# A two-layer decoder step on one Trainium2 core: queries of the other tokens by rows from weights already in the ring, and the samples' second-layer projections in four quarters of a PSUM bank

## The chip, the cores and the metric

The program runs on one core of a Trainium2 chip. The metric is the device time of one execution in microseconds (us): 2491.01 us as the median of three runs before the change (2483.01 to 2494.72). The names of the engines in the rows are PE (TensorE, the matrix engine; PEld is its weight load, that is, the loading of the stationary operand), DVE (VectorE), ACT (ScalarE), POOL (GpSimd, which here issues the gathers of the experts' rows) and SP (SyncE, which issues the other loads and the stores). All data are 32-bit floats. A 32-bit matrix multiplication stands in the trace as two PE records, a transpose as one.

## What is computed

256 prompt tokens and 8 x 4 sample tokens go through two layers with width 1024. Layer 0 mixes by a gated recurrence and sparse attention, layer 1 by dilated attention; each is followed by an expert layer, whose routing is the part that matters here:

```python
def peer_ffn(x, w_q, sub_keys, u, v):                 # 16 blocks of 128 query columns
    q = (xt @ w_q).reshape(n, PEER_HEADS, 2, PEER_QDIM // 2)      # w_q: 1024 x 2048
    s = jnp.einsum('nhcd,hckd->nhck', q, sub_keys)                # scores against 128 keys
    s1, i1 = lax.top_k(s[:, :, 0], PEER_TOPK); s2, i2 = lax.top_k(s[:, :, 1], PEER_TOPK)
    ...                                               # 16 of the 16 x 16 pairs, for each of 8 heads
    eidx = jnp.take_along_axis(cidx, sel, axis=-1); gate = jax.nn.softmax(top, axis=-1)
    ...                                               # 128 experts a token: gelu(u[e].x) * gate, times v[e]

def odd_project(x, pos, w_in):                        # layer 1: w_in is 1024 x 3072
    h = (x @ w_in).reshape(B, T, 3, DIL_HEADS, HEAD_DIM)
    return rope(h[:, :, 0], pos), rope(h[:, :, 1], pos), h[:, :, 2]
```

## The kernel before, in words

The tokens are three tiles: two of 128 prompt tokens (tiles 0 and 1) and one of 32 samples (tile 2). `k.x` holds them by rows, `k.xT` transposed: eight chunks of 128 of the width on the partitions, the tokens along the free axis (samples first). A projection multiplies chunk by chunk and sums eight chunks in a PSUM bank.

The program has three parts. First comes the mixer of layer 0 up to its output projection and normalisation (`even_out`). The second part is the routing of tile 0. It is two blocks with a barrier behind each: in the first, `project_cols` makes the queries of tile 0 (`peer_q0`); in the second, `route` scores and selects for tile 0 on DVE (`first_route`), while `project_cols` makes the queries of the samples and of tile 1 (`rest`, named `peer_q12`). `project_cols` keeps the *weights* stationary: for each of 16 blocks of 128 query columns and each chunk it loads a 128x128 piece of the weights and streams 32 or 128 tokens against it; the result is already transposed, as `route` wants it (`peer_qT`), and leaves by a copy, in `rest` by ACT alone. The weights lie in the eight slots of the experts' ring (`uv`, 1 MB each); `rest` loads all eight again. In this block ACT runs its part of `rest` first and then the one exponential of `first_route` (`scalar=(rest, first_route)`), for which DVE waits before it can finish the softmax, the expert numbers (`slots`) and the gates. PE runs the scores of `first_route`, then `rest`.

The third part is one long block, in which the 576 expert steps run in the foreground and everything else beside them. A step gathers 128 rows of 8 KB, one for each token, into a ring of eight slots (L1769, issued by POOL), takes the dot products on DVE (L1787), scales a diagonal on ACT and multiplies it into the sum on PE (L1879, four records), or, for some of the steps, sums on DVE (L1801). The slot is free when the sum has read it. The side work (routings of the other tiles, and per tile a `mixer`: layer 1's projection, rotation, attention and output, then the projection of the layer-1 queries) is cut into ticks with weights; `WINDOWS` says between which steps each runs, and the ticks of a window are spread over its steps in proportion to their weights. The instructions of an engine therefore stand in one fixed order, expert steps and side ticks mixed, and each waits for the one ahead of it. A side stage ends on a barrier of the four engines with SP, and SP issues the loads of the next stage before it lets them on.

In `mixer 2` (the samples; steps 408 to 498) the stages that concern us are: `project_wide` with the samples (32 tokens) stationary, which streams 512 columns of weights at a time into six banks of 32 used partitions (L502), twelve loads of 1 MB; `rotate_and_store`, which rotates queries and keys in four pieces of 32x512 (L706 to L711) and stores keys and values; `transposes` of sixteen 32x128 blocks; then four attention stages over the cached keys and values, the output projection, and `late_routing`, which projects the samples' queries with `project_wide` again (eight loads of 1 MB, four banks) and transposes sixteen blocks.

Of the kernel before, what the change touches and what calls it, by code (L numbers as in the profile page):

```python
# [32 lines left out]
D = 1024  # L33
KC = D // 128
# [189 lines left out]
def cols(t):  # L224
    return slice(COL0[t], COL0[t] + ROWS[t])
# [296 lines left out]

def project_cols(k, name, w, n, outT, wbuf, toks=(slice(0, NTOK),), banks=ALL_BANKS, by=("vector", "scalar")):
# [62 lines left out]
    for side, engine in enumerate(by):  # L586
        stage.on(engine)(lambda eng, side=side, engine=engine: take_out(eng, side, outs[side], copies[engine]))
    return stage
# [1400 lines left out]
def dilated_tile(k, name, t, a, o, val, kT):  # L1989
# [5 lines left out]
    with ExitStack() as outer:  # L1995
# [3 lines left out]
        with ExitStack() as inner:  # L1999
            qk = k.sbuf(name + "_qk", [128, 1, 2 * D], ctx=inner)  # L2000
            with ExitStack() as load:
# [5 lines left out]
                stages.append(project_wide(k, name + "_in", a["odd_w_in"][0], ((0, 2 * D), (2 * D, D)), out, wbuf, t, SIDE_BANKS))  # L2007
            with ExitStack() as rot:
                tmp = k.sbuf(name + "_tmp", [128, 4, 256], ctx=rot)
                stages.append(rotate_and_store(k, name + "_rot", qk, val, tiles, o["dil_p"], o["dil_s"], tmp))  # L2010
            groups = [([qk[0:r, 0, at + 128 * (c + j):at + 128 * (c + j + 1)] for j in range(4)], dst[:, c:c + 4, cols(t)])
                      for dst, at in ((qT, 0), (kT, D)) for c in range(0, HP, 4)]
            stages.append(transposes(k, name + "_qk", groups, SIDE_BANKS))
# [26 lines left out]
def late_routing(k, name, t, a, route_tile):  # L2040

    r = ROWS[t]
    with ExitStack() as late:
        qT = k.sbuf(name + "_qT", [128, 2 * PH, r], ctx=late)
        keysT = k.sbuf(name + "_keysT", [128, 2 * PH, NK], ctx=late)
        with ExitStack() as load:
# [4 lines left out]
            stages = [turn_keys(k, name + "_keys", a["peer_sub_keys"][1], keys, keysT, SIDE_BANKS),  # L2051
                      project_wide(k, name + "_q", a["peer_w_q"][1], ((0, 2 * PH * 128),), lambda j: rows[0:r, 512 * j:512 * (j + 1)],
                                   wbuf, t, SIDE_BANKS),
                      transposes(k, name + "_qT", [([rows[0:r, 128 * (4 * i + j):128 * (4 * i + j + 1)] for j in range(4)],
                                                    qT[:, 4 * i:4 * i + 4, :]) for i in range(4)], SIDE_BANKS)]
# [32 lines left out]
def build(nc, a, o):  # L2088
    with ExitStack() as whole:
# [6 lines left out]
        with ExitStack() as ctx:  # L2096
# [16 lines left out]
            with ExitStack() as first:  # L2113
# [60 lines left out]
```

## Time and profile before

| | |
|---|---|
| median of three runs | 2491.01 us |
| the runs | 2483.01 to 2494.72 us |
| span of the profiled execution, first to last instruction | 2536.6 us |
| mean granted TensorE clock | 0.845 of 2.4 GHz |
| busy: PE, DVE, ACT, POOL | 77%, 58%, 22%, 29% |
| moved by DMA | 759.29 MB, mean 299 GB/s |

The profiled execution has no time of its own beside its span here; the span is 45.6 us (1.8%) longer than the median of the runs without the profiler. Busy shares are means over stages with different limits, so the page is read by stage: its second part cuts the span into 40 slices of 63.4 us. PEclk is the granted clock in tenths of 2.4 GHz, and DMA is the busy share of the 16 DMA engines; up to 1.02 stands for full in the windows, where they move about 420 GB/s.

### The profile page before, as it was taken

To read this page: it belongs to the slowest core of one execution; us is meant where nothing else is said; L and a number is where in the kernel's file an instruction comes from. 1 tells how busy PE (TensorE), PEld (TensorE's weight loads), DVE (VectorE), ACT (ScalarE), POOL (GpSimd) and SP (SyncE) were. 2 spreads that over 40 slices of the span, in tenths; PEclk is the share of its full clock that TensorE was granted. 3 is DMA by queue.
4 is the path that set the end of the run, shared out by engine and by line. 5 is a ranking of instruction groups with operands and counts; after the bars stand their busy time and mean duration, and the time that the engine had idled before them with its cause. 6 is when DMAs were issued, how large, how long until landed. Compare 5 with 4: busy or idle time off the path is not lost.

```text
span 2536.6 us, 20142 instructions
## 1 busy us (share of the span) xinstructions
PE 1965.3 (77%) x6151; PEld 987.9 (39%) x6151; DVE 1470.2 (58%) x3338; ACT 559.8 (22%) x1759; POOL 728.6 (29%) x612
## 2 busy tenths in 40 slices
PE   7968289889877877886869768677978687878776
PEld 3456255569833322222324223233422255623221
DVE  0043632128078777657755973585594565456976
ACT  0010222000022322224322231142221122212231
POOL 4000000000044455433444452233442132223442
PEclk9985556685599999998989988888999787789988
DMA  8200100524199999999999999799999799889997
GB/s 277 91 17 1 37 1 0 152 81 133 40 422 421 421 421 422 399 419 359 401 413 421 415 395 420 307 384 383 406 393 405 278 359 349 325 329 384 402 385 306
DMA packets 160436, 759.29 MB, mean 299 GB/s; under 512 B 22204, under 2 KB 63048, under 8 KB 80328
## 3 DMA queue, kind: packets, MB, share of 16 engines
q0 software_dynamic: 84480, 608.21, 59.0%
q1 hardware_dynamic: 75848, 149.80, 16.4%
q8 instruction: 49, 0.80, 0.1%
q14 instruction: 59, 0.48, 0.1%
HBM read 752.35 MB, written 5.60 MB: 299 GB/s over the span
## 4 chain that ended last, share of the span: by engine, by line
DMA 23%; PE 20%; DVE 17%; issue 6%; ACT 2%; SPq 1%; PEld 1%; POOL 1%; PEldq 1%; DVEq 1%; ACTq 0%; POOLq 0%
DMA uv<-in_experts_dram,slots 16%; PE ps L1879 9%; DVE uv L1787 6%; PE ps L502 4%; PE ps L824 2%; DMA sample_cache<-in_odd_w_in_dram 1%; PE ps L796 1%; DMA last_w<-in_odd_w_in_dram 1%; DMA sample_w<-in_peer_w_q_dram 1%; PE ps L657 1%; POOL uv L1769 1%; SPq L1494 1%; PEldq L1915 1%; DVE acc L1801 1%; ACT diag L1855 1%
## 5 line engine op out<-in xcount | busy, mean ns | idle before, releaser
L1769 POOL DMA_INDIRECT uv<-in_experts_dram,slots x576 | 698.0, 1212 | 1746.5 <-PE ps L1879 1000.9
L1879 PE MATMUL ps<-uv,diag 128*128 128x512 f32 (+1 forms) x1880 | 973.5, 659 | 271.1 <-ACT diag L1855 211.9
L1787 DVE CUSTOM_DVE_ANT_0 uv<-uv,x 128x1024 f32<-128x1024 f32 x512 | 623.0, 1225 | 307.3 <-DMA uv<-in_experts_dram,slots 253.8
L1879 PEld LDWEIGHTS ps<-uv,diag 128*128 128x128 f32 (+1 forms) x1880 | 349.2, 198 | 813.3 <-issue 469.2
L1833 ACT ACTIVATE gelu<-dot 128x2 f32<-128x2 f32 x288 | 58.6, 203 | 1051.4 <-DVE dot L1787 1045.9
L1855 ACT ACTIVATE diag<-const,wgt 128x128 f32<-128x128 f32 (+1 forms) x470 | 165.0, 387 | 9.4
L1842 ACT ACTIVATE wgt<-gate,gelu 128x1 f32<-128x1 f32 x576 | 138.0, 286 | 48.2 <-SPq L1982 14.4
L563 PE MATMUL ps<-xT,uv 128*128 128x128 f32 (+1 forms) x768 | 139.0, 367 | 1.6 <-DMA uv<-in_peer_w_q_dram 1.6
L563 PEld LDWEIGHTS ps<-xT,uv 128*128 128x128 f32 x768 | 138.7, 287 | 1.8 <-DMA uv<-in_peer_w_q_dram 1.8
L1801 DVE SCALAR_TENSOR_TENSOR acc<-uv,wgt,acc 128x1024 f32<-128x1024 f32 x101 | 129.3, 1280 | 1.5 <-ACT wgt L1842 1.5
L1787 DVE CUSTOM_DVE_ANT_0 uv<-uv,xs 128x1024 f32<-128x1024 f32 x64 | 78.0, 1225 | 74.7 <-DMA uv<-in_experts_dram,slots 73.3
L425 PE MATMUL ps<-even_w,xT 128*128 128x512 f32 (+3 forms) x240 | 99.0, 565 | 6.1 <-issue 4.9
L502 PE MATMUL ps<-last_w,xT 128*128 128x512 f32 x160 | 76.2, 620 | 13.4 <-DMA last_w<-in_odd_w_in_dram 12.5
L502 PE MATMUL ps<-first_w,xT 128*128 128x512 f32 x160 | 75.4, 611 | 2.9 <-DMA first_w<-in_odd_w_in_dram 2.9
L425 PEld LDWEIGHTS ps<-even_w,xT 128*128 128x128 f32 (+1 forms) x240 | 38.0, 165 | 66.7 <-issue 62.6
L440 DVE COPY h<-ps 128x512 f32<-128x512 f32 (+3 forms) x8 | 5.0, 626 | 89.6 <-PE ps L425 56.5
L502 PEld LDWEIGHTS ps<-last_w,xT 128*128 128x128 f32 x160 | 30.8, 196 | 55.7 <-issue 36.2
L502 PE MATMUL ps<-sample_cache,xT 128*32 128x512 f32 x96 | 46.1, 627 | 8.1 <-DMA sample_cache<-in_odd_w_in_dram 8.1
L657 PE MATMUL ps<-even_w_out,xT 128*128 128x512 f32 (+1 forms) x96 | 44.3, 624 | 6.5 <-DMA even_w_out<-in_even_w_out_dram 6.5
L878 DVE COPY xT<-ps 128x256 f32<-128x256 f32 (+3 forms) x19 | 6.8, 360 | 72.1 <-PE ps L824 72.0
L502 PEld LDWEIGHTS ps<-first_w,xT 128*128 128x128 f32 x160 | 29.7, 193 | 47.7 <-issue 41.4
L824 PEld LDWEIGHTS ps<-sample_s_probT,sample_cache 128*128 128x128 f32 x256 | 47.4, 290 | 2.1 <-issue 2.1
(409 smaller groups left out, 1911.6 us busy)
## 6 DMA issues: line engine op xcount, KB each, us to landing
uv<-in_peer_w_q_dram SPq DMA_DIRECT2D x16, 1024.0 KB, 11.9
sample_cache<-in_cache_dil_kv_dram SPq DMA_DIRECT2D x64, 256.0 KB
first_w<-in_odd_w_in_dram SPq DMA_DIRECT2D x12, 1024.0 KB
last_w<-in_odd_w_in_dram SPq DMA_DIRECT2D x12, 1024.0 KB, 12.0
sample_cache<-in_odd_w_in_dram SPq DMA_DIRECT2D x12, 1024.0 KB, 15.6
uv<-in_experts_dram,slots POOLq DMA_INDIRECT x576
even_w<-in_even_w_in_dram SPq DMA_DIRECT2D x8, 1024.0 KB, 8.4
first_w<-in_peer_w_q_dram SPq DMA_DIRECT2D x8, 1024.0 KB, 9.7
```

Source lines behind the costliest of these rows:

```text
L425: last = nc.tensor.matmul(k.bank(banks[i % nb])[0:ROWS[t], 0:widths[j]], k.xT[:, 4 * half + c, cols(t)], wbuf[:, load % slots, c, 0:widths ...
L502: last = nc.tensor.matmul(k.bank(banks[job])[0:r, :], k.xT[:, chunk, cols(t)], wbuf[:, i % slots, width * c + 512 * j:width * c + 512 * (j ...
L563: last = nc.tensor.matmul(k.bank(banks[i % nb])[:, place], wbuf[:, j % slots, c, 128 * (i % 2):128 * (i % 2 + 1)], k.xT[:, c, tok], start= ...
L657: last = nc.tensor.matmul(bank(n, h)[0:ROWS[t], :], catT[:, 2 * i + c, cols(t)], w[:, i % slots, c, 512 * h:512 * (h + 1)], start=(i == 0 ...
L824: last = nc.tensor.matmul(out, lhsT, pick(probT[0:kn, r % 2, :]), start=start, stop=stop, skip_group_check=True)
L1769: self.k.nc.gpsimd.indirect_dma_start(out=self.uv[:, s % RING, :], out_offset=None, in_=self.table, in_offset=bass.IndirectOffsetOnAxis(ap ...
L1787: ins = nc.vector.tensor_tensor_reduce(self.uv[:, s % RING, 0:D], self.uv[:, s % RING, 0:D], x, 1.0, 0.0, ALU.mult, ALU.add, self.dot[:, g ...
L1801: nc.vector.scalar_tensor_tensor(self.acc[:, :], v, w, self.acc[:, :], ALU.mult, ALU.add).then_inc(self.added, 1)
L1833: nc.scalar.activation(self.gelu[:, grp % 2, :], self.dot[:, grp % 2, :], ACT.Gelu).then_inc(self.gelued, 1)
L1842: ins = nc.scalar.activation(self.wgt[:, grp % 2, g:g + 1], self.gate[:, t, j:j + 1], ACT.Copy, scale=self.gelu[:, grp % 2, g:g + 1])
L1855: last = nc.scalar.activation(self.diag[:, step % RING, 0:w], k.c(shape), ACT.Copy, scale=self.wgt[:, grp % 2, g:g + 1])
L1879: last = nc.tensor.matmul(k.bank(c)[0:m, :], self.diag[:, s % RING, 0:m], self.uv[:, s % RING, D + 512 * c:D + 512 * (c + 1)], start=(j == ...
```

## The change

There are two parts.

In the routing of tile 0, `rest` becomes `queries_by_rows`. It loads nothing: the weights that `peer_q0` left in the ring are used. The *tokens* are now stationary. Tile 1 takes 32 multiplications with 512 columns into banks 4 to 7 (four banks of rows, eight chunks each). The samples take 32 multiplications of 32 stationary columns and 512 streamed ones, all into bank 4: the four quarters of the query columns go to the partitions 0 to 31, 32 to 63, 64 to 95 and 96 to 127, chunk by chunk with the four quarters next to each other. ACT copies the five results to SBUF; PE turns them by 16 and 4 transposes of 128x128; ACT copies those to `peer_qT`, four copies and four.

In `mixer 2` and in the late routing of the samples, `project_wide` becomes `project_quarters` in the same manner: queries and keys of layer 1 (2048 columns) go to four quarters of one bank by 32 multiplications with 512 columns, the values (1024 columns) to four quarters of a second bank by 32 with 256, and the late queries to one bank by 32 with 512. The loads are the same twelve and eight of 1 MB. The rotation runs once over 128x512, the keys and values leave by three stores, and four transposes of 128x128 with eight small copies take the place of sixteen transposes with four copies. The ticks and weights of these stages change with them.

```diff
+def project_quarters(k, name, w, groups, leaves, wbuf, banks):
...
+    stage = Stage(k, len(ticks), 1.4)
...
+                for q in range(4):
+                    last = nc.tensor.matmul(k.bank(banks[g])[NS * q:NS * (q + 1), 0:n], k.xT[:, chunk, SMP],
+                                            wbuf[:, i % slots, width * c + n * q:width * c + n * (q + 1)],
+                                            start=(chunk == 0), stop=(chunk == KC - 1), skip_group_check=True)
...
+def turn_quarters(k, name, rows, outs, banks):
...
+        for m in range(4):
+            last = nc.tensor.transpose(k.bank(banks[m // 2])[:, 128 * (m % 2):128 * (m % 2 + 1)], rows[:, 128 * m:128 * (m + 1)],
+                                       k.c("ident"))
...
+def rotate_and_store_quarters(k, name, qk, val, out_s, tmp):
...
+        rotate(k, qk[:, :], qk[:, :], (2, 128), HEADS // 2, tmp)
...
+        for j in range(2):
+            k.store(sp, dst[:, 0, 512 * j:512 * (j + 1)], qk[NS * (2 + j):NS * (3 + j), :])
+        k.store(sp, dst[:, 1, :], val[0:NS, 2, :])
+        k.wait_for_stores(sp)
...
+def queries_by_rows(k, name, wbuf, rows, quarters, qT):
...
+        for j in range(4):
+            for c in range(KC):
+                last = nc.tensor.matmul(wide(4 + j), k.xT[:, c, cols(1)], wbuf[:, 2 * j:2 * j + 2, c, :], start=(c == 0), stop=(c == KC - 1))
+            last.then_inc(made, 1)
+        pe.wait_ge(taken, 1)
+        for c in range(KC):
+            for q in range(4):
+                last = nc.tensor.matmul(wide(4, slice(NS * q, NS * (q + 1))), k.xT[:, c, SMP], wbuf[:, 2 * q:2 * q + 2, c, :],
+                                        start=(c == 0), stop=(c == KC - 1), skip_group_check=True)
+        last.then_inc(made, 1)
+        for i, b in enumerate((5, 6, 7, 4)):
+            pe.wait_ge(taken, i + 2)
+            for j in range(4):
+                last = nc.tensor.transpose(k.bank(b)[:, 128 * j:128 * (j + 1)], rows[:, 512 * i + 128 * j:512 * i + 128 * (j + 1)], ident)
+            last.then_inc(made, 1)
...
+        for j in range(4):
+            act.wait_ge(made, j + 1)
+            copy(rows[:, 512 * j:512 * (j + 1)], k.bank(4 + j)).then_inc(taken, 1)
...
-                    first_route, rest = r(0, 0, qT, keysT, load, None), project_cols(
-                        k, "peer_q12", a["peer_w_q"][0], 2 * PH * 128, qT, wbuf, (SMP, cols(1)), (4, 5, 6, 7), ("scalar",))
+                    rows = k.sbuf("peer_rows", [128, 2 * PH * 128], ctx=load)
+                    quarters = k.sbuf("peer_quarters", [128, 512], ctx=load)
+                    first_route = r(0, 0, qT, keysT, load, None)
+                    rest = queries_by_rows(k, "peer_q12", wbuf, rows[:, :], quarters[:, :], qT)
                     alone(k, first_route, rest, scalar=(rest, first_route))
```

On PE, in the block of the first routing, the program before has this behind the scores (`peer_keysT,peer_qT`); the last two rows stand 32 times in turn. The first row is tile 0's queries, the branches are the barrier; `uv` is the ring, `xT` the tokens.

```order
L563 MATMUL ps<-xT,uv 128x128 x128
L274 UNCONDITIONAL_BRANCH
L275 UNCONDITIONAL_BRANCH
L1573 MATMUL ps<-peer_keysT,peer_qT 128x128 x16
L563 MATMUL ps<-xT,uv 128x32 x4
L563 MATMUL ps<-xT,uv 128x128 x4
```

The same place on PE now:

```order
L692 MATMUL ps<-xT,uv 128x128 x128
L274 UNCONDITIONAL_BRANCH
L275 UNCONDITIONAL_BRANCH
L1756 MATMUL ps<-peer_keysT,peer_qT 128x128 x16
L736 MATMUL ps<-uv,xT 128x512 x32
L741 MATMUL ps<-uv,xT 32x512 x32
L747 MATMUL ps<-const,peer_rows 128x128 x16
L751 MATMUL ps<-const,peer_quarters 128x128 x4
```

256 multiplications and 16 hand-overs to ACT have become 64 and 20 transposes.

On ACT, in the same block, what stands ahead of the exponential of the first routing (`route_e`) is now this; before it were 32 copies of 128x32 and 128x128.

```order
L760 COPY peer_rows<-ps 128x512 x4
L762 COPY peer_quarters<-ps 128x512
L765 COPY peer_qT<-ps 128x4x128 x4
L768 COPY peer_qT<-ps 128x4x32 x4
L1777 ACT_TABLE_LOAD
L1777 ACTIVATE route_e<-route_e 128x128
```

The exponential still stands behind the whole of `rest`.

On DVE, in `mixer 2`, the rotation of the samples (`sample_qk` with `sample_tmp`) before stood in four pieces, two of them between expert steps (`uv,dot<-uv,x` is a step's dot product); the first piece and the step behind it:

```order
L706 TENSOR_TENSOR sample_tmp<-sample_qk,const 32x256
L707 TENSOR_TENSOR sample_tmp<-sample_qk,const 32x256
L708 TENSOR_TENSOR sample_tmp<-sample_qk,const 32x256
L709 TENSOR_TENSOR sample_tmp<-sample_qk,const 32x256
L710 TENSOR_TENSOR sample_qk<-sample_tmp 32x8x32
L711 TENSOR_TENSOR sample_qk<-sample_tmp 32x8x32
L1787 ISA uv,dot<-uv,x 128x1024
L1787 ISA dot 128x1
```

Now it is one piece, and what follows is this (the step's two `ISA` rows stand twice there and are shown once):

```order
L893 TENSOR_TENSOR sample_qk<-sample_tmp 128x8x32
L894 TENSOR_TENSOR sample_qk<-sample_tmp 128x8x32
L638 MEMSET progress 128x1
L1970 ISA uv,dot<-uv,x 128x1024
L1970 ISA dot 128x1
L1984 SCALAR_TENSOR_TENSOR acc<-uv,wgt,acc 128x1024
L620 COPY sample_qT<-ps 128x64 x2
L620 COPY dil_kT<-ps 128x2x32 x2
```

24 rotation instructions became six, and the expert steps that lay between them moved: on DVE 429 dot products stood ahead of the first copy of the turned cache keys (`sample_s_kTs`), now 426, and each of the four attention stages has 13 steps where it had 12.

## Rows read from the trace of the kernel before

**Rows 1.** The page's second part: DMA in 40 slices of the span.
```profile
DMA  8200100524199999999999999799999799889997
```
**Rows 2.** Windows by stage; columns: stretch, length, busy by engine, clock, DMA share, GB/s.
```profile
510.00:523.00 13.00, 13.00 (x32) 3.40 (x32) 6.40 (x9) 0.20 (x1) 0.00 (x0) 1.00 1.00 320
553.00:571.00 18.00, 17.39 (x156) 17.23 (x155) 1.46 (x5) 1.32 (x5) 0.00 (x0) 1.00 0.00 1
...
587.00:685.00 98.00, 98.00 (x460) 97.98 (x460) 38.28 (x146) 4.95 (x28) 0.00 (x0) 0.50 0.11 34
```
**Rows 3.** Timeline of DVE, first routing; columns: start, us, engine, line, operation, [idle before].
```profile
626.12 0.29 DVE L1663 TENSOR_TENSOR route_e<-route_top 128x128 f32<-128x128 f32 x1
687.31 0.29 DVE L1666 TENSOR_REDUCE route_den<-route_e 128x8 f32<-128x128 f32 x1 [60.90 <-ACT route_e L1594]
```
**Rows 4.** Timeline of ACT, end of the first routing's block.
```profile
685.68 1.28 ACT L1594 ACT_TABLE_LOAD   x1
686.97 0.31 ACT L1594 ACTIVATE route_e<-route_e 128x128 f32<-128x128 f32 x1
```
**Rows 5.** Timeline of PE, first routing's block.
```profile
570.88 3.81 PE L1573 MATMUL ps<-peer_keysT,peer_qT 128*128 128x128 f32 x32 [0.61 <-PEq L274]
576.30 108.97 PE L563 MATMUL ps<-xT,uv 128*128 128x32 f32 x512 [1.62 <-DMA uv<-in_peer_w_q_dram]
```
**Rows 6.** Timeline of PE: 512 columns against 32, and transposes, at full clock.
```profile
1930.21 5.34 PE L502 MATMUL ps<-sample_cache,xT 128*32 128x512 f32 x12
...
2078.44 1.91 PE L348 MATMUL ps<-const,sample_cache 128*128 128x128 f32 x16
```
**Rows 7.** Timeline of PE: neighbours that write different halves of the partitions.
```profile
245.21 1.97 PE L1114 MATMUL ps<-hg_v_b,hg_keyT 32*64 32x512 f32 x4
...
1681.37 1.13 PE L824 MATMUL ps<-last_p_probT,dil_val 128*64 128x128 f32 x8 [3.59 <-ACT last_p_probT L899]
```
**Rows 8.** The clock in the windows of rows 7.
```profile
245.20:247.20 2.00, 1.98 (x5) 0.29 (x4) 0.00 (x0) 0.00 (x0) 0.00 (x0) 0.50 0.00 0
...
1681.00:1682.60 1.60, 1.23 (x9) 0.90 (x10) 0.87 (x2) 1.58 (x2) 0.00 (x0) 0.50 1.00 415
```
**Rows 9.** Groups by line and form: copies, rotation; columns: busy, mean ns.
```profile
L359 ACT COPY sample_s_kTs<-ps 128x512 f32<-128x512 f32 x16 | 9.1, 571 | 3.9 <-PE ps L348 2.3 <-issue 1.6
...
L707 DVE TENSOR_TENSOR sample_tmp<-sample_qk,const 32x256 f32<-32x256 f32 x4 | 1.7, 420 | 0.0
```
**Rows 10.** Windows of mixer 2; columns as in rows 2.
```profile
1940.00:1960.00 20.00, 17.15 (x39) 3.93 (x37) 3.66 (x5) 1.09 (x4) 4.07 (x4) 1.00 1.01 419
...
1980.00:2000.00 20.00, 13.87 (x27) 4.15 (x24) 16.13 (x32) 4.13 (x11) 4.58 (x5) 0.83 0.36 127
2000.00:2020.00 20.00, 8.32 (x23) 4.19 (x24) 15.10 (x30) 2.79 (x11) 4.05 (x4) 0.59 0.86 310
...
2040.00:2200.00 160.00, 131.32 (x545) 85.97 (x545) 93.90 (x159) 39.28 (x110) 46.24 (x40) 0.80 0.91 352
...
2300.00:2320.00 20.00, 14.97 (x46) 4.78 (x44) 8.20 (x13) 3.49 (x12) 5.97 (x6) 1.00 0.85 330
1900.00:2340.00 440.00, 342.99 (x1099) 165.64 (x1098) 247.86 (x439) 95.60 (x279) 119.22 (x104) 0.84 0.88 346
```
**Rows 11.** Timeline of PE around the samples' rotation.
```profile
1984.42 3.62 PE L502 MATMUL ps<-sample_cache,xT 128*32 128x512 f32 x8
...
2026.81 1.96 PE L348 MATMUL ps<-const,sample_cache 128*128 128x128 f32 x8 [5.75 <-SPq L1982]
```
**Rows 12.** Timeline of SP's queue there.
```profile
1963.79 0.37 SPq L476 DMA_DIRECT2D sample_cache<-in_odd_w_in_dram  x1
...
2011.68 3.98 SPq L336 DMA_DIRECT2D sample_cache<-in_cache_dil_kv_dram  x8
2015.71 10.94 SPq L1494 DMA_DIRECT2D sample_cache<-in_cache_dil_kv_dram  x8
```

**Rows 13.** The page's sixth part: issue, KB, median us from issue to landing.
```profile
sample_cache<-in_odd_w_in_dram SPq DMA_DIRECT2D x12, 1024.0 KB, 15.6
```

More of the change, by code:

```diff
@@ new lines, in turn_quarters, with _, take_out @@
+def turn_quarters(k, name, rows, outs, banks):
+    nc = k.nc
+    turned, v_out, s_out = [k.sem(name, n) for n in ("turned", "v_out", "s_out")]
+    stage = Stage(k, 2, 1.5)
+    sides = ((v_out, nc.vector.tensor_copy), (s_out, nc.scalar.copy))
+    @stage.on("tensor")
+    def _(pe):
+        for m in range(4):
+            last = nc.tensor.transpose(k.bank(banks[m // 2])[:, 128 * (m % 2):128 * (m % 2 + 1)], rows[:, 128 * m:128 * (m + 1)],
+                                       k.c("ident"))
+            if m % 2:
+                last.then_inc(turned, 1)
+        yield
+        yield
+    def take_out(eng, side):
+        done, copy = sides[side]
+        yield
+        eng.wait_ge(turned, side + 1)
+        for first, n, dst in outs:
+            src = k.bank(banks[side])[:, 0:256].rearrange("p (m j t) -> p j m t", m=2, t=NS)
+            for j in range(n):
+                last = copy(dst[:, 4 * j + 2 * side:4 * j + 2 * side + 2, :], src[:, first + j])
+        last.then_inc(done, 1)
+        yield
+    stage.on("vector")(lambda dve: take_out(dve, 0))
+    stage.on("scalar")(lambda act: take_out(act, 1))
+    return stage
@@ L1999, in dilated_tile @@
         with ExitStack() as inner:
-            qk = k.sbuf(name + "_qk", [128, 1, 2 * D], ctx=inner)
+            qk = k.sbuf(name + "_qk", [128, 1, 512 if t == 2 else 2 * D], ctx=inner)
             with ExitStack() as load:
@@ L2050, in late_routing @@
             keys = rows[:, :].rearrange("p (a b) -> p a b", b=128)
[L2051 to L2055, printed above, removed]
+            turned = turn_keys(k, name + "_keys", a["peer_sub_keys"][1], keys, keysT, SIDE_BANKS)
+            if t == 2:
+                quarters = rows[:, 0:512]
+                stages = [turned, project_quarters(k, name + "_q", a["peer_w_q"][1], ((0, 2 * PH * 128),), ([(quarters, slice(0, 128), 512)],),
+                                                   wbuf, SIDE_BANKS),
+                          turn_quarters(k, name + "_qT", quarters, [(0, 2, qT[:, 0:8, :]), (2, 2, qT[:, 8:16, :])], SIDE_BANKS)]
+            else:
+                stages = [turned,
+                          project_wide(k, name + "_q", a["peer_w_q"][1], ((0, 2 * PH * 128),), lambda j: rows[0:r, 512 * j:512 * (j + 1)],
+                                       wbuf, t, SIDE_BANKS),
+                          transposes(k, name + "_qT", [([rows[0:r, 128 * (4 * i + j):128 * (4 * i + j + 1)] for j in range(4)],
+                                                        qT[:, 4 * i:4 * i + 4, :]) for i in range(4)], SIDE_BANKS)]
         with ExitStack() as inner:
```

116 lines of the change are left out of this document (111 added, 5 removed).

## The prediction

> **What bounds the kernel now.** I read the page's slices first [rows 1]. From slice 12 on, DMA stands at 9 nearly throughout: the expert steps run at the rate of their gathers there, and a faster PE buys nothing. Two kinds of holes matter. One lies ahead of the experts, in slices 10 and 11 (571 to 698 us), where DMA is at 4 and 1: the first routing. The others lie at slices 32, 35 and 36 (7, 8 and 8), in mixer 2. The windows then price both. In the first routing PE is busy all of 98 us at a clock of 0.50, while DVE works 38 [rows 2]. The timelines show who ends last: DVE has route_e at 626.4 and stands 60.90 us for ACT's exponential [rows 3]; ACT comes to it only behind the last copy of `rest`, at 685.7 [rows 4]; and ACT was kept by PE, whose 512 records run from 576.30 to 685.27 [rows 5]. Nothing else runs, and POOL's first gather stands behind the barrier. So that block ends by PE, and every us taken from PE there is a us of the kernel, until DVE's own end.
>
> In mixer 2 the DMA share is 1.01 while most of the weights come in, then 0.36 and 0.86 around the rotation, 0.91 in the attention stages and 0.85 at the end of the late queries [rows 10]. Over the 440 us it is 0.88 against the 1.01 of full, so (1.01 - 0.88) x 440 = 57 us of DMA time are unused. This is all that the second part of the change can win.
>
> **Part one: the first routing.** The reload of 8 MB and its wait of 1.62 us at 576.30 go. PE is free at 570.88 + 3.81 = 574.7 [rows 5]. What a record costs: 512 columns against 32 stationary ones at full clock take (5.34 - 0.2) / 12 = 0.427 us (0.2 being the last one's tail, my estimate), a transpose (1.91 - 0.2) / 16 = 0.107 us [rows 6]. The width of the stationary side does not enter: on the 98 us a 32-column stream costs as much as a 128-column one, 108.97 / 512 = 0.213 us at half clock [rows 5], which is 0.427 for 256 such columns and so agrees with 0.427 for 512 at full clock.
> - Tile 1: 32 multiplications, 64 records x 0.427 = 27.3 us, to 602.0.
> - Samples: 64 records. One after the other they would be 27.3 us too; four at a time 16 x 0.427 = 6.8 us, to 608.9. Before has no case of four, but of two. Four records of 512 columns at half clock (0.85 us each, 3.4 in a row) took 1.97 us there, and eight of 128 (0.213 each, 1.7) took 1.13, these with all 128 rows of the array in use [rows 7], both at a clock of 0.50 [rows 8]. So pairs that write different partitions overlap nearly whole. Bounds: 6.8 and 27.3 us; I take 6.8, since both pairs halve.
> - The end: behind the quarters a copy of the samples' rows, then four to `peer_qT`, 0.571 us each [rows 9], in ACT's order, then four small copies of about 0.3: 0.2 + 5 x 0.57 + 1.1 = 4.2 us, to about 613. The 20 transposes (2.1 us, 4.3 at half clock) lie beside the copies.
>
> DVE is not touched and has route_e at 626.4. `rest` then ends 13 us under that cover. The table load of 1.28 us stood ahead of the wait, not behind it [rows 4], so it is done by then too; the exponential of 0.31 us follows at once, and DVE goes on at about 626.8 instead of 687.31. Gain: 60.5 us. What is late next is DVE itself. The bounds come from the clock and the overlap, in the rivals below.
>
> The Trainium skill has a rule against this (TensorE: Matmul & The Clock Gate, "Part 3: Packing small matmuls"): weight loads overlap running multiplications only when the row group differs, and the quarters share all rows. The trace disagrees: neighbours with the same rows overlap [rows 7]. The same section gives 2.38x for three column tiles; with it as an estimate the samples would take 27.3 / 2.38 = 11.5 us, and the sum would be the same, since 4.7 us more fit under DVE.
>
> **Part two: mixer 2 and the samples' late queries.** 160 records x 0.427 = 68.3 us on PE (96 and 64 of them) become 17.1 if four overlap. Most of it buys nothing, because the DMA is full there. What the chain gives:
> - Projection. The last piece of weights is asked for at 1963.79; its multiplications end at 1984.42 + 3.62 = 1988.0 [rows 11, 12]. A piece takes 15.6 us to land [rows 13], so it is there at about 1979.4. What is left behind it, at a quarter of its length and with an expert step between, ends near 1982: -6 us. Bounds 0 (the norm of the expert layer that falls there binds) and -10.
> - Rotation: 24 instructions x 0.41 become 6 [rows 9]; DVE does 128 partitions in the time of 32. 18 x 0.41 = -7.4 us on the chain, since PE and the cache loads wait for it. Bounds -5 and -10 (two expert steps between the pieces go too).
> - Transposes behind it: 0. They are fewer, but SP issues the keys' and values' loads from 2011.68 until 2026.65 in any case [rows 12], and PE goes on at 2026.81, when SP lets it [rows 11]. This wait takes the place of what is saved. The third store goes beside the others: 0.4 us.
> - Late queries: DMA is full up to 2300, then 0.85 for 20 us [rows 10]: -4 us, bounds 0 and -8.
> - Moved steps: each attention stage now has 13 expert steps for 12. PE works 131 of 160 us there and DMA has a share of 0.91 [rows 10], so a step (1 MB, 2.5 us of DMA) fits in part: +1 us a stage, +4 in all; bounds 0 and +8.
>
> Sum, rounded: -6 - 7 - 4 + 4 = -13 us, bounds -28 (all lower ends) and +3 (all upper ends).
>
> **The forecast.** -60.5 - 13 = -73.5 us. Against the profiled execution that is 2536.6 - 73.5 = 2463 us of span. The runs without profiler are 1.8% shorter; PE at a fixed clock should not depend on that, so I take the us as they are: 2491.0 - 73.5 = 2417.5, rounded to 2417 us.
>
> **The rivals.**
> 1. The quarters run one after the other. This is what the skill's rule would make of them here. For it: no row shows four at once, each streaming over all 128 rows. Against: the pairs [rows 7]. `rest` then ends at 613 + 20.5 = 634, 7.5 us behind DVE, a gain of 53 us. In mixer 2 only rotation and the ends remain, about -9. 2491 - 53 - 9 = 2429 us.
> 2. The clock falls to 1.2 GHz (0.50) in the block of the first routing. For it: before it was 0.50 there over 98 us of unbroken PE work, behind 1.00 in the stage ahead [rows 2]. Against: that work was 128- and 32-column streams; with 512-column streams of 32 stationary columns the clock was 1.00 [rows 2], as in mixer 2's projection [rows 10]. With overlap: 574.7 + 54.6 + 13.7 + 6 = 649, 22.5 us late, gain 38: 2491 - 38 - 13 = 2440 us.
> 3. Part two gives nothing, since the DMA in front of and behind the hole takes the time back: 2491 - 60.5 = 2430 us. For it: rows 10 with DMA full on both sides; against: the 0.36 in the middle.
> 4. The other side: quarters in a row and at half clock, everywhere. `rest` ends at 574.7 + 54.6 + 54.6 + 7 = 691, 5 us later than before; in mixer 2 160 records at 0.85 instead of 0.43 add 68 us to a PE that is busy 17 of 20 us [rows 10], some +50. 2491 + 5 + 50 = 2546 us. In the first block the sign turns where a record takes over 0.8 us in the mean, (685 - 575 - 7) / 128. Both conditions together have [rows 2, 7] against them.
>
> **Chances.** Forecast (overlap, full clock, part two between -5 and -28) 0.62; rival 1 0.10; rival 2 0.09; rival 3 0.16; rival 4 0.03. The likeliest's own range is 2402 to 2426; with the rivals 1 to 3 and what the profiled execution cannot tell, the range is 2398 to 2439. Under 0.5% (12 us) this kernel cannot be told from no change. Cases 1 to 3 and the forecast are all faster by more: 0.95 faster; a partial form of rival 4 could land within: 0.03; slower 0.02.
>
> **What would show it.** In the changed profile: DVE's idle before the reduction of route_e under 1 us (60.90 before), and the first gather some 60 us earlier; the 32-column records of the first routing ending four by four within about 0.9 us of each other, and the clock 1.00 there; no loads of peer_w_q in that block; the samples' projection ending some 18 us after its last piece is asked for instead of 24; one rotation of 2.5 us; the window between projection and first cache keys shorter by some 13 us, the DMA share of 0.36 gone. The forecast is wrong if DVE waits for ACT by more than 5 us (rival 1 or 2, told apart by clock and spacing), or if mixer 2's window is as long as before (rival 3).

## The result, and the profile after

| | before | after |
|---|---|---|
| median, 19 runs each side by side | 2501.21 us | 2474.75 us |
| lowest to highest | 2483.01 to 2552.04 | 2468.65 to 2488.82 |
| span of the profiled execution | 2536.6 us | 2474.0 us |
| PE records | 6151 | 5795 |

2417 us had been forecast, with a range of 2398 to 2439; the changed kernel takes 2474.75. The kernel before has two groups of runs: 10 of the 19 lie from 2483 to 2501 us, 9 from 2529 to 2552. The changed kernel has one. Against the lower group alone the change is 0.6% faster: the ratio is 0.9939, with an interval of 0.9922 to 0.9956, which is 15 us (11 to 19). The profile shown ahead of the prediction is one execution of the upper group, and everything below turns on it.

The page of the changed kernel, its slices of the clock and of DMA (compare [rows 1]):

```profile
PEclk9986556699899999988899989898997776778988
DMA  8200100340999999989999999899999988889997
```

The first routing on PE (compare [rows 5]), ACT [rows 4] and DVE [rows 3], and its window [rows 2]:

```profile
565.20 3.81 PE L1756 MATMUL ps<-peer_keysT,peer_qT 128*128 128x128 f32 x32 [0.61 <-PEq L274]
568.85 27.63 PE L736 MATMUL ps<-uv,xT 128*128 128x512 f32 x64
```
```profile
L741 PE MATMUL ps<-uv,xT 128*32 128x512 f32 x64 | 7.1, 594 | 0.0
```
```profile
606.02 0.82 ACT L768 COPY peer_qT<-ps 128x128 f32<-128x128 f32 x4
606.86 1.28 ACT L1777 ACT_TABLE_LOAD   x1
620.75 0.31 ACT L1777 ACTIVATE route_e<-route_e 128x128 f32<-128x128 f32 x1 [12.61 <-DVE route_e L1846]
```
```profile
620.42 0.29 DVE L1846 TENSOR_TENSOR route_e<-route_top 128x128 f32<-128x128 f32 x1
621.09 0.29 DVE L1849 TENSOR_REDUCE route_den<-route_e 128x8 f32<-128x128 f32 x1 [0.38 <-ACT route_e L1777]
```
```profile
565.00:610.00 45.00, 40.62 (x180) 19.80 (x180) 40.83 (x205) 6.92 (x14) 0.00 (x0) 1.00 0.00 1
```

The experts' gathers fill the slices from number 11 on, one slice earlier. Inside this block every step came as forecast. The samples' records start four at a time, 5 to 8 ns after one another, with some 410 ns between one four and the next. Tile 1 takes 27.6 us, the samples' 64 records 7.1 (forecast 6.8), the clock is 1.00, ACT stands 12.61 us for DVE (forecast 13 under cover), and DVE's idle of 60.90 us is 0.38. Against the profiled execution of before, 60.5 us are gone, and yet the runs gained 15.

### The profile page after: what moved, and what is told of

Its sections match the earlier page's. It is cut to its first block, busy times and chain, and to the rows that moved or that the text cites. A ratio compares the mean times of both kernels' runs of the same rounds, so it can differ in the third digit from the quotient of the medians.

```text
span 2474.0 us, 19380 instructions
## 1 busy us (share of the span) xinstructions
PE 1858.3 (75%) x5795; PEld 889.4 (36%) x5795; DVE 1463.7 (59%) x3323; ACT 557.7 (23%) x1741; POOL 720.7 (29%) x612
## 4 chain that ended last, share of the span: by engine, by line
DMA 26%; PE 21%; DVE 17%; issue 5%; ACT 2%; SPq 1%; POOL 1%; PEldq 1%; DVEq 1%; PEld 0%; ACTq 0%; POOLq 0%
DMA uv<-in_experts_dram,slots 18%; PE ps L2062 11%; DVE uv L1970 6%; PE ps L502 3%; PE ps L1007 2%; DMA sample_cache<-in_odd_w_in_dram 2%; DMA last_w<-in_odd_w_in_dram 2%; PE ps L979 2%; PE ps L840 1%; DMA sample_w<-in_peer_w_q_dram 1%; DVE acc L1984 1%; ACT diag L2038 1%; DVE route_ef L1841 1%; DMA out_dil_p_dram<-dil_val 1%; POOL uv L1952 1%
## 5 line engine op out<-in xcount | busy, mean ns | idle before, releaser
L1952 POOL DMA_INDIRECT uv<-in_experts_dram,slots x576 | 690.1, 1198 | 1692.2 <-PE ps L2062 1017.7
L1007 PEld LDWEIGHTS ps<-sample_s_probT,sample_cache 128*128 128x128 f32 x256 | 52.6, 317 | 3.3 <-issue 3.3
L1007 PE MATMUL ps<-sample_s_probT,sample_cache 128*128 128x8 f32 x256 | 51.5, 345 | 0.0
L1034 DVE TENSOR_TENSOR nsa_prob<-ps,const 128x512 f32<-128x512 f32 (+3 forms) x16 | 10.2, 640 | 68.6 <-PE ps L979 68.6
L1970 DVE DVE_READ_ACCUMULATOR2_ANT dot<- 128x1 f32 x576 | 47.2, 82 | 0.0
L979 PE MATMUL ps<-sample_s_kTs,sample_q_b 128*64 128x256 f32 x128 | 35.1, 429 | 15.9 <-DVE sample_q_b L1685 15.9
```

Source lines behind the costliest of these rows:

```text
L979: last = nc.tensor.matmul(score_bank(i)[p0:p0 + pn, c0:c0 + cn], lhsT, rhs, start=start, stop=stop)
L1007: last = nc.tensor.matmul(out, lhsT, pick(probT[0:kn, r % 2, :]), start=start, stop=stop, skip_group_check=True)
L1952: self.k.nc.gpsimd.indirect_dma_start(out=self.uv[:, s % RING, :], out_offset=None, in_=self.table, in_offset=bass.IndirectOffsetOnAxis(ap ...
L1970: ins = nc.vector.tensor_tensor_reduce(self.uv[:, s % RING, 0:D], self.uv[:, s % RING, 0:D], x, 1.0, 0.0, ALU.mult, ALU.add, self.dot[:, g ...
```

## The experiments

Each kernel ran on one chip beside runs of the kernel before. A run over 2515 us is called long and the others short: among the 94 runs of the kernel before none lies between 2507 and 2525 us.

### Where the 60 us are

Four kernels, the kernel before again among them (its expectation has the two counts of the 19 runs exchanged). `p1_only` is part one of the change alone, `p2_only` part two alone. `no_reload` is the kernel before without its second 8 MB of loads and the waits for them:

```diff
-        for j in range(slots):
+        for j in range(0 if kept else slots):
             load(sp, j)
...
-            if i % 2 == 0:
+            if i % 2 == 0 and not kept:
                 pe.wait_ge(landed[j % slots], 16 * (j // slots + 1))
```

> The kernel before, unchanged, to get the profile of one of its shorter executions. Its 19 runs fall in two groups, 9 of 2483 to 2501 us and 10 of 2529 to 2552 us; the profile shown (2536.6 us) is of the longer group. Theory A (clock in the first routing): in the shorter group the queries of the samples and of tile 1 run at a granted clock of 1.00, the 512 PE records take 55 to 60 us in place of 108.97 us, DVE waits 2 to 15 us in place of 60.90, and the loop of the experts behind it is as long as in the shown profile (1847 us within 5). Theory B (the loop): the clock of that block is 0.50 in every run, and the 45 us lie in the loop of the experts, which is then about 1800 us.

> The kernel before without the second load of the 8 MB of layer 0's query weights: the same instructions on PE, with no wait for a load. It tells what brings the low clock in that block. Theory A1 (the waits for the reload, in which PE stands still, let the clock fall): all runs in the shorter group, clock 1.00 in the block, about 2484 us. Theory A2 (the stream itself, 128x128 pieces of weights against 32 and 128 columns in turn, does not hold the clock): two groups of runs as before, or all in the longer one. Theory B: no difference from before.

> The changed kernel with the second part undone (dilated_tile and late_routing as before): queries by rows only. Theory A: against the shorter runs of before it gains what `rest` ends behind DVE at full clock, 5 to 10 us: 2479 to 2485 us, and no run in a longer group. Theory B (part one is worth its 60 us in every run, part two costs about 45 us): 2425 to 2435 us. If part two gives nothing in the loop, this kernel is as long as the whole change, 2475 us within 5.

> The changed kernel with the first part undone (the first routing as before): quarters in the samples' second-layer projections only. Theory A: two groups of runs as before, the shorter one within 5 us of before's shorter one (2485 to 2495 us). Theory B: part two costs about 45 us, 2535 us and more against the shorter runs of before. My forecast had -13 us for this part (2476 us in the shorter group).

The kernel before, another execution of it (span 2481.1 us), in PE's and DVE's timeline (compare [rows 5] and [rows 3]) and in a window of the same stage (compare [rows 2]):

```profile
564.10 3.81 PE L1573 MATMUL ps<-peer_keysT,peer_qT 128*128 128x128 f32 x32 [0.61 <-PEq L274]
569.43 57.44 PE L563 MATMUL ps<-xT,uv 128*128 128x32 f32 x512 [1.52 <-DMA uv<-in_peer_w_q_dram]
```
```profile
628.91 0.28 DVE L1666 TENSOR_REDUCE route_den<-route_e 128x8 f32<-128x128 f32 x1 [9.31 <-ACT route_e L1594]
```
```profile
590.00:600.00 10.00, 10.00 (x92) 10.00 (x91) 9.69 (x53) 1.06 (x6) 0.00 (x0) 1.00 0.02 5
```

The same 512 records took 57.44 us at a clock of 1.00 where they had taken 108.97 at 0.50, and DVE waited 9.31 us instead of 60.90. These 51.5 us are most of the 55.5 us between the spans. Another 6.8 lie ahead of the scores (564.10 against 570.88), 5.5 of them ahead of tile 0's queries and 1.3 in these, and the loop behind gives 3 back. So the two levels of the clock in this block make the difference between this short execution and the long one. The runs that have no profile show their mean clock alone, and it parts them in the same way: it is 0.855 to 0.867 in 25 short runs of before, and 0.835 to 0.849 in 49 long ones. In the lower group part one can give 9.31 - 0.38 = 8.9 us.

| kernel | runs to 2515 us: n, median | runs from 2515 us |
|---|---|---|
| before, 11 runs here | 2, 2497.2 | 9 |
| before_again | 3, 2489.8 | 3 |
| p1_only | 6, 2486.6 | 0 |
| p2_only | 5, 2480.6 | 1 |
| no_reload | 6, 2486.2 | 0 |

`no_reload` computes with the same narrow streams and has no long run; in its profile the 512 records take 57.34 us at a clock of 1.00.

### What of the reload lets the clock fall

The reload is a wait of 1.5 us at the start of the block, and a traffic of 8 MB behind it. `reload_first` loads and awaits piece 0 alone, `reload_late` pieces 3 to 7, which PE reaches some 20 us later; `reload_two` waits for two pieces at the start. They differ from the kernel before in

```diff
-        for j in range(slots):
+        for j in range(slots) if loaded is None else loaded:
             load(sp, j)
...
-            if i % 2 == 0:
+            if i % 2 == 0 and (loaded is None or j in loaded):
                 pe.wait_ge(landed[j % slots], 16 * (j // slots + 1))
+                if loaded is not None and j == 0:      # reload_two alone
+                    pe.wait_ge(landed[1], 16)
```

with `loaded` (0,), (3, 4, 5, 6, 7) and (0, 1) for `peer_q12`. `after_wait` is the changed kernel with 1 MB reloaded and awaited ahead of its first multiplication:

```diff
+        sp.dma_start(wbuf[:, 0, :, :], w_first).then_inc(landed, 16)
...
+        pe.wait_ge(landed, 16)
         for j in range(4):
             for c in range(KC):
```

> The kernel before, whose second making of queries loads only the first of its eight pieces again (1 MB) and waits for it alone: the wait of PE at the start of it stays (1.5 us), the traffic of the other 7 MB goes. Theory A1 (the wait makes the clock fall in some executions): two groups again, about half of six runs over 2515 us, the others near 2488. A2 (the traffic of 8 MB does): no run over 2500. A3 (neither; what differs lies ahead of this block, and the absence of long runs without the reload was chance): two groups.

> The kernel before, whose second making of queries loads the last five of its eight pieces again (5 MB), which PE comes to some 20 us later: traffic stays, the wait of PE at the start goes. A1 (the wait makes the clock fall): no run over 2500 us, all near 2486. A2 (the traffic does) or A3 (neither): two groups, about half of the six runs over 2515 us. With the run beside it: only the first in two groups is A1, only the second A2, both A3, neither means that it takes both or that the cause is rarer than six runs show.

> The kernel before, loading the first two pieces again and waiting for both before the first multiplication: the wait of PE at that place grows from 1.5 us to about 4. With one piece 4 of 6 runs were long. Theory A1 (the wait there is what lets the clock fall): at least as many long runs, 4 to 6 of 6 over 2530 us. Rival (a wait of any length is not the cause, and 0 of 18 without it was chance): no more than 2 of 6.

> The changed kernel, whose second making of queries loads the first 1 MB of the weights again and lets PE wait for it, as before did: one wait of 1.5 to 1.8 us on PE between the scores and the first multiplication; the other traffic stays away. Theory A1 (that wait makes the clock fall to 0.50 for the rest of the block in more than half of the executions, whatever PE multiplies): two groups of runs. Where the clock stays, the wait lies under DVE's 12.6 us of cover and the run takes the changed kernel's 2475 us; where it falls, the 64 records of tile 1 take 54.6 us and the quarters 14, ACT's exponential comes 20 to 28 us behind DVE's need, and the run takes 2495 to 2505 us, about half of the six runs. Rival (the clock falls only under streams of 32 and 128 columns): all six at the changed kernel's time.

| kernel | PE's wait there | streams | long runs of all |
|---|---|---|---|
| before, five sets of runs | 1.62 and 1.52 us | 32 and 128 columns | 58 of 93 |
| p2_only, p2_beside | 1.77 and 1.53 | the same | 6 of 18 |
| reload_first | 1.50 | the same | 4 of 6 |
| reload_two | 4.67 | the same | 6 of 6 |
| no_reload, reload_late | none | the same | 0 of 6, 0 of 12 |
| after_wait | 1.69 | 512 columns | 0 of 6 |
| changed kernel, four sets of runs | none | 512 columns | 0 of 43 |
| p1_only, p1_beside | none | 512 columns | 0 of 18 |

(One more run of before, at 3165 us and a mean clock of 0.545, belongs to neither group and is left out.) `reload_two`, PE's timeline and windows (clock last but two), then DVE's:

```profile
568.44 3.81 PE L1575 MATMUL ps<-peer_keysT,peer_qT 128*128 128x128 f32 x32 [0.61 <-PEq L274]
576.91 109.57 PE L565 MATMUL ps<-xT,uv 128*128 128x32 f32 x512 [4.67 <-DMA uv<-in_peer_w_q_dram]
```
```profile
565.00:575.00 10.00, 6.64 (x58) 6.28 (x56) 4.09 (x11) 0.27 (x1) 0.00 (x0) 1.00 0.57 175
575.00:580.00 5.00, 3.09 (x14) 3.12 (x15) 4.83 (x31) 0.00 (x0) 0.00 (x0) 0.68 0.22 69
580.00:600.00 20.00, 20.00 (x96) 20.00 (x95) 19.38 (x115) 1.06 (x6) 0.00 (x0) 0.50 0.00 1
600.00:680.00 80.00, 80.00 (x378) 80.00 (x376) 23.28 (x59) 4.20 (x24) 0.00 (x0) 0.50 0.00 1
```
```profile
688.52 0.28 DVE L1668 TENSOR_REDUCE route_den<-route_e 128x8 f32<-128x128 f32 x1 [64.59 <-ACT route_e L1596]
```

And `reload_first` and `p2_only`, in profiled executions that are short ones, with waits of the same length:

```profile
567.52 57.44 PE L563 MATMUL ps<-xT,uv 128*128 128x32 f32 x512 [1.50 <-DMA uv<-in_peer_w_q_dram]
568.24 57.44 PE L692 MATMUL ps<-xT,uv 128*128 128x32 f32 x512 [1.77 <-DMA uv<-in_peer_w_q_dram]
```

The long runs need the wait and not the traffic: with 5 MB of traffic and no wait at the start none of 12 is long, with 1 MB and the wait 4 of 6 are. That a longer wait makes more of them is likely but not shown: at the rate of before, six of six would come by chance once in 17 times. The long runs take the narrow streams too: the rival to A1 in `after_wait` held, six runs of 2466 to 2481 us. (A fall shorter than DVE's 12.6 us of cover would not show in them.) So part one removes the long runs twice over. The Trainium skill also has a clock that falls where PE waits for a DMA (TensorE: Matmul & The Clock Gate, "HAM oscillation — how this bites in real kernels"). The waits of its example are longer than the 1.5 to 1.8 us here, so the runs agree with it in kind, and go beyond it. The picture in Part 1 of the same page, of a clock that comes back once PE is busy, does not fit here: the 109.57 us that follow are without a gap, at 0.50 to the end. Why a wait of 1.5 to 1.8 us does it in some executions and not in others stays open. Its length does not decide: the clock fell behind 1.62 us and held behind 1.77.

### The quarters, and the order of the multiplications

`serial_quarters` is the changed kernel with the two loops of the samples exchanged, for the first routing alone:

```diff
-        for c in range(KC):
-            for q in range(4):
+        for q in range(4):
+            for c in range(KC):
                 last = nc.tensor.matmul(wide(4, slice(NS * q, NS * (q + 1))), ...
```

> The changed kernel, whose samples in the first routing are multiplied quarter by quarter: all eight chunks of a quarter, then the next quarter, so that neighbours write the same partitions; the same 32 multiplications in another order. Theory Q (four neighbours overlap because they write different quarters of the partitions): the 64 records take 27.3 us where they took 7.07, ACT comes 7 to 8 us behind DVE, the first dot product and the run come 7 to 8 us later, 2482 us. Rival R (a matmul with 32 stationary columns is fast by itself, in any order): 7 us, and the changed kernel's time.

Its timelines of PE, ACT and DVE:

```profile
593.64 22.59 PE L741 MATMUL ps<-uv,xT 128*32 128x512 f32 x64
616.17 1.97 PE L747 MATMUL ps<-const,peer_rows 128*128 128x128 f32 x16
```
```profile
616.27 0.59 ACT L762 COPY peer_quarters<-ps 128x512 f32<-128x512 f32 x1 [21.94 <-PE ps L741]
```
```profile
621.25 0.28 DVE L1849 TENSOR_REDUCE route_den<-route_e 128x8 f32<-128x128 f32 x1 [3.27 <-ACT route_e L1777]
```

The same 32 multiplications take 22.59 us where they took 7.07: Q holds, and R is refuted. The size was off. I had expected 27.3 and a DVE 7 to 8 us late; it is 2.9 us later than in the changed kernel (3.27 against 0.38), and the four runs have a median of 2475.1 us against 2471.8. Why 22.59 us is 17% less than 64 x 0.427 stands in the start times of the single records. Neighbours of the same quarter start about 430 ns apart and save nothing. Around each of the three changes of quarter four records start only 6 to 30 ns behind the one ahead of them, so there too pairs ran side by side: 12 x 0.427 = 5.1 us. Against the Trainium skill's rule that weight loads overlap only between row groups (TensorE: Matmul & The Clock Gate, "Part 3: Packing small matmuls"), four neighbours that share all 128 rows run 27.3 / 7.07 = 3.9 times as fast as in a row.

### What part two gives, and where it goes

`after_again`, `after_beside` and `after_third` are the changed kernel, `p1_beside` and `p2_beside` its halves once more, all as references. `same_steps` and `same_steps_again` are the changed kernel with the weights of before for the ticks of part two, which gives each attention stage 12 expert steps again:

```diff
-    stage = Stage(k, len(ticks), 1.4)
+    stage = Stage(k, len(ticks), (25 if len(groups) == 2 else 17) / len(ticks))
...
-    stage = Stage(k, 2, 1.5)
+    stage = Stage(k, 2, 3.75)
...
-    stage = Stage(k, 1, 2.5)
+    stage = Stage(k, 1, 10.0)
```

> The changed kernel once more, on the chip of the three runs below it. Theory A (its gain lies in part in the absence of the long group of runs, and of the 12 us that part two gains by step 433 it gives back most in the attention stages): all runs in one group between 2465 and 2490 us, median about 2475, none over 2500; profile with first dot product at 631.5 us and the attention stages done at about 1412 us (step 450) to 1549 (step 480) behind it, as in its first profile. Rival (single group by chance): at least one of the six runs over 2515 us.

> The changed kernel with the ticks' weights of before in the samples' second mixer (projection 25 and 17 over its ticks, turning 3.75, rotation 10), so that the attention stages have 12 expert steps each again and stand at the same steps. Theory B (what part two gains by step 433 is given back because each attention stage got a 13th expert step): the loop is 8 to 12 us shorter than that of the changed kernel, median 2463 to 2467 us. Rival C (the DMA takes the time back whichever step stands where, since it is full in front and behind): within 4 us of the changed kernel, 2471 to 2479. Rival D (the new weights were better): slower by 5 to 10 us.

> The changed kernel beside the next three, on the same chip: 2474 to 2477 us median, no run over 2500 us.

> The changed kernel with the ticks' weights of before in the samples' second mixer, once more, beside the changed kernel. Its first six runs had a median of 2469.8 us against 2476.4 of the changed kernel on that chip. Theory B (the 13th expert step in each attention stage costs): again 5 us or more below the run beside it, 2467 to 2471. Rival C (the steps' places don't matter, the first difference was the scatter of six runs): within 3 us of the run beside it.

> The changed kernel beside its two halves on one chip, so that the 15 us between the undisturbed runs of before and of the changed kernel can be split: 2472 to 2477 us, no run over 2500.

> Part one alone (the first routing by rows, mixer 2 as before). If part two is worth 7 us (the traces' steps 408 to 500) to 12 us (the difference of the medians of other chips), this stands 7 to 12 us above the changed kernel, 2481 to 2487 us, with no run over 2515. Rival: part two gives nothing, the same as the changed kernel within 3 us.

> Part two alone (mixer 2 and the late queries in quarters, the first routing as before). Where the clock holds in the first routing, part one is worth 7.7 us by the trace (first dot product 639.2 against 631.5): the short runs stand 5 to 8 us above the changed kernel, 2480 to 2484 us; the wait at the start of the block is still there, so one or more of six runs over 2515 us.

| short runs: n, median | chip of the first halves | chip of the second |
|---|---|---|
| before (with before_again) | 5, 2495.1 | 10, 2488.2 |
| part one alone | 6, 2486.6 | 12, 2480.0 |
| part two alone | 5, 2480.6 | 7, 2486.9 (and 5 long) |
| both | not run there | 10, 2471.5 |

Part one alone gives 8.5 and 8.3 us, as the trace has it (8.9); part two alone gives 14.5 and 1.4, and on top of part one 8.5. Medians of a few runs scatter too much for it, so I took it from the traces: the loop's time from expert step 408 to 500, which holds all of mixer 2. It is 415.2 us in the mean of seven executions without part two (407.8 to 428.4) and 408.6 in eight with it and the changed weights (406.8 to 410.4): -6.6 us. This is a mean and no more. The two executions of the kernel before itself (407.8 and 409.9) lie where those with part two lie, and without the highest of the seven, `p1_only`'s 428.4 (the longest of its six runs), it is -4.4. The runs bear the size out: 11 to 19 us in all, less 8.9 for part one, leave 2 to 10.

SP's queue shows where time is won and lost. The kernel before (short execution), from the first weights of the projection to the first cache keys and the first weights of the late queries:

```profile
1860.97 47.60 SPq L476 DMA_DIRECT2D sample_cache<-in_odd_w_in_dram  x12
1949.52 0.36 SPq L175 DMA_DIRECT2D out_dil_s_dram<-sample_qk  x1
...
1954.05 3.98 SPq L336 DMA_DIRECT2D sample_cache<-in_cache_dil_kv_dram  x8
...
2206.28 35.74 SPq L476 DMA_DIRECT2D sample_w<-in_peer_w_q_dram  x8
```

On DVE, the first and last row of its rotation (24 instructions, with two steps between the pieces):

```profile
1936.96 0.41 DVE L706 TENSOR_TENSOR sample_tmp<-sample_qk,const 32x256 f32<-32x256 f32 x1
...
1948.96 0.41 DVE L711 TENSOR_TENSOR sample_qk<-sample_tmp 32x256 f32<-32x256 f32 x1
```

The same two views of the changed kernel (six instructions):

```profile
1852.74 46.80 SPq L544 DMA_DIRECT2D sample_cache<-in_odd_w_in_dram  x12
1921.44 0.82 SPq L175 DMA_DIRECT2D out_dil_s_dram<-sample_qk  x2
...
1927.52 4.67 SPq L336 DMA_DIRECT2D sample_cache<-in_cache_dil_kv_dram  x8
...
2201.80 34.08 SPq L544 DMA_DIRECT2D sample_w<-in_peer_w_q_dram  x8
```
```profile
1919.07 0.42 DVE L889 TENSOR_TENSOR sample_tmp<-sample_qk,const 128x256 f32<-128x256 f32 x1
...
1920.87 0.42 DVE L894 TENSOR_TENSOR sample_qk<-sample_tmp 128x256 f32<-128x256 f32 x1
```

From weights to cache keys it was 93.1 us and is 74.8. From there to the late queries it was 252.2 and is 274.3. Over the seven and the eight executions, and the two of `same_steps`:

| means, us | without part two | with it | same_steps, its two executions |
|---|---|---|---|
| first weights to first cache keys | 93.9 | 75.5 | 82.4, 81.1 |
| from there to the late queries | 256.3 (249.9 to 266.1) | 274.7 (272.9 to 275.8) | 268.4, 258.9 |
| from there to step 500 | 62.9 (61.0 to 68.0) | 56.5 (55.7 to 59.0) | 58.9, 60.1 |
| gathers in the first two | 17 and 60 | 15 and 64 | 17 and 60 |

So 18.4 us are won and 18.4 given back, with 79 steps in the time of 77. What is left over stands in the third stretch, which has two steps fewer and the late queries in quarters. With its steps as before (`same_steps`) it is 59.5 in the mean of two. So about half of the 6.4 us there is the late queries' and half the two steps'.

The windows of the second stretch and of 408 us from the first weights on, the kernel before and the changed kernel (columns as in [rows 2]):

```profile
1954.00:2206.00 252.00, 199.77 (x748) 120.74 (x748) 143.06 (x235) 58.12 (x166) 68.12 (x60) 0.78 0.86 330
1861.00:2269.00 408.00, 318.12 (x1020) 156.31 (x1020) 217.76 (x358) 82.80 (x244) 103.59 (x91) 0.82 0.88 341
```
```profile
1927.50:2202.00 274.50, 208.62 (x745) 125.41 (x745) 151.12 (x248) 60.15 (x176) 73.89 (x64) 0.75 0.85 321
1853.00:2261.00 408.00, 285.53 (x1040) 148.63 (x1041) 211.24 (x343) 80.68 (x245) 108.99 (x92) 0.74 0.88 343
```

A step takes 252 / 60 = 4.2 us there before and 274.5 / 64 = 4.3 after, and the DMA share stays at 0.86 and 0.85. In the first stretch it rose, from 0.83 to 0.86 without part two to 0.94 to 0.97 with it: the hole around the rotation is mostly filled. `same_steps` asked whether the moved steps are a loss. Its first six runs (median 2469.8 against 2476.4 beside it) spoke for it, the second six (2471.8 against 2471.8) did not. Over both, its mean is 1.3 us lower, with an interval from 5.6 lower to 3.5 higher, which leaves out the 8 to 12 us of theory B; C (within 4 us) is in keeping with it. With no step moved the attention stages still took 263.6 us in the mean where they had taken 256.3. So the 18.4 given back are not all the price of moved steps; what the other part is was not isolated, and two executions are few for it.

## Why the prediction was wrong

**The step that failed** is in "The forecast": "PE at a fixed clock should not depend on that, so I take the us as they are: 2491.0 - 73.5". The clock was not fixed. 2491.0 is the median of three runs in which these records take 57.4 us, and 60.5 us is the price in an execution in which they take 109. The subtraction mixed the two. Part one was worth 8.9 us to the runs that it was subtracted from, and not 60.5. Within the upper group the sum holds to 6 us: the 9 runs of it beside the changed kernel have a median of 2535.87 us, and less 60.5 and 6.6 that is 2468.8, against 2474.4 measured over all 43 runs of the changed kernel. Within the lower group the sum is 2491.0 - 8.9 - 6.6 = 2475.5, against 2474.75; that it comes so close is luck, given the scatter of the 6.6.

The sign of it stood in the rows. The profile's span was 42 us over the slowest of the three runs shown (2494.72), though a span lies 1.8 us under its own run (2474.0 against 2475.81). And a clock of 0.50 under unbroken PE work [rows 2] names a stretch that at the other level would be shorter by half of 108.97 us [rows 5], 54 us, near the 42 to 54 us by which that span exceeds the three runs. I read the 45.6 us as a cost of profiling spread over the span.

**Part one, the block itself:** right in each step (overlap, order of ACT's copies, table load, DVE's end). Priced at full clock the gain of 60.5 us is 60.5 - 51.5 = 9.0 us; 8.9 were measured. Rival 1, the quarters in a row, is refuted by the 7.07 us. Rival 2, that the clock falls in the changed block, did not happen in 43 runs; its mechanism was at work in the kernel before. (Its own price, 2440 us, lies just outside the range of 2398 to 2439 that was to hold it.)

**Part two, -13 forecast, -6.6 in the traces:** the bounds (-28 to +3) hold it.
- Projection, -6 forecast: from the first weights' load to the rotation it was 1936.96 - 1860.97 = 76.0 us and is 1919.07 - 1852.74 = 66.3, so -9.7, within the bounds. Two steps have left that stretch; in `same_steps`, where they stand in it, it is 70.1 and 69.1, so about -7.
- Rotation, -7 forecast: with the steps between its pieces it was 12.4 us (1936.96 to 1949.37) and is 2.2, so -10.2, just past the bound. DVE takes 0.42 us for 128 partitions and took 0.41 for 32. From its end to the first keys' load, where the third store was to cost 0.4, it is 6.2 us for 4.7, +1.5.
- Moved steps, +4 forecast, bounds 0 and +8: the attention stages took 18.4 us more, and this is the place where the sum of part two is short by 6.4. Two fewer steps ahead of them and two fewer behind them stand against that. `same_steps` does not show that moving steps costs more than the forecast 4: without it the loop from step 408 to 500 takes 411.7 and 402.9 us against 408.6. With no step moved the stages were still 7.3 us longer in the mean of two (268.4 and 258.9 against 249.9 to 266.1), and for that the sum had no term. Its cause stays open.
- Transposes 0, and SP's issue in their place: from the first keys' load to the first transpose of them it was 14.1 us (1954.05 to 1968.17) and is 15.1 (1927.52 to 1942.60), so the saved transposes win nothing. PE now waits there 10.80 us for the keys to land, where it had waited 7.01 for SP. Late queries -4: about -3 by the third stretch of `same_steps`, from two executions.

**Rival 3**, that DMA takes part two back, is half right: all 18.4 us won by the first cache load are given back up to the late queries, part of them to four more steps. That it is DMA that takes the rest is argued from its share of 0.85 there, and not shown.

## What to carry to other kernels

Before a wait is priced from a profile, its execution has to be placed among the runs: a span off by more than the few us between profile and run means another state, and then each term is priced at the clock of the runs that it is subtracted from. A short wait of PE ahead of a long stretch of narrow multiplications can cost the whole stretch a factor of two in some executions; keep the weights that are already there, or stream wide. In a loop with foreground steps, a stage that became shorter does not tell the gain: here 18.4 us won in one were given back in the next. Measure between two fixed steps of the loop, in several executions.

## What the runs showed of the hardware

- The granted clock stayed at 0.50 through 108.97 and 109.57 us of unbroken PE work (`before`, `reload_two`), and was 1.00 in other executions of the same instructions (57.44 us).
- Four neighbouring multiplications of 32 stationary columns that share all 128 rows and write four quarters of a bank's partitions overlap 3.9 times (7.07 us for 64 records); one quarter after the other takes 22.59 us for the same work, and overlaps only where the quarter changes.
- With 32.6 us less PE work in mixer 2 (318.12 to 285.53 us of 408), the mean clock there fell from 0.82 to 0.74. It was 0.79 to 0.83 in eight executions without part two and 0.74 to 0.76 in eight with it. Most of the fall lies between the first weights and the first cache keys (0.88 to 0.89, then 0.69 to 0.74). Less work on PE and a lower clock went together, and so part of what was taken off PE came back; how much was not isolated.
